# A 64-expert layer in 26 passes instead of 28: experts of different widths share a pass, and the first product moves ahead

## The reference, cut to what matters

```
scores = sigmoid(h @ w_router)                      # 64 experts
idx = top_k(scores + b_router, 8)                   # 8 experts for each token
gate[t, e] = 2.5 * scores / sum over the 8, else 0
hid = silu(h @ w_exp_gate[e]) * (h @ w_exp_up[e])   # 1024 -> 256
routed = sum_e (hid * gate[:, e]) @ w_exp_down[e]   # 256 -> 1024
ffn = routed + (silu(h @ w_sh_gate) * (h @ w_sh_up)) @ w_sh_down
```

## Time and profile before

| what | value |
|---|---|
| median of three runs | 949.46 us |
| the profiled execution's own time | 951.25 us |
| its span in the profile | 949.1 us |
| mean granted TensorE clock | 0.947 |
| TensorE busy (matmul) | 819.6 us |
| bytes moved by DMA | 279.98 MB |

### The profile page before, as it was taken

The page is one execution under the profiler, slowest core; times in us unless marked ns, Lnnn a source line. Parts: engine busy times, 40 slices in busy tenths (PEclk is TensorE's granted clock), DMA queues, the critical chain, the costliest instruction groups (busy, mean ns, idle before and its releaser), DMA issues.

```text
span 949.1 us, 10498 instructions
## 1 busy us (share of the span) xinstructions
PE 819.6 (86%) x3946; PEld 447.9 (47%) x3946; DVE 317.5 (33%) x656; ACT 154.8 (16%) x269; POOL 69.8 (7%) x64
## 2 busy tenths in 40 slices
PE   1699969988899999799999899899799897939882
PEld 0388448544455444675535445453454352505340
DVE  2120586666654427622222212212121121202116
ACT  1212342111112311211111101111111010101111
POOL 0000123344320000300000000000000000000000
PEclk9889979999999999899999989999899898969997
DMA  8962422556565277668699999999999999899901
GB/s 289 385 211 98 168 89 89 189 189 233 189 242 204 87 264 287 245 238 352 240 423 422 420 422 420 421 422 420 421 422 421 421 421 417 365 421 422 366 1 44
DMA packets 68001, 279.98 MB, mean 295 GB/s; under 512 B 8912, under 2 KB 10960, under 8 KB 43120
## 3 DMA queue, kind: packets, MB, share of 16 engines
q1 hardware_dynamic: 63888, 270.56, 71.6%
q0 software_dynamic: 2144, 5.84, 1.8%
q10 hardware_dynamic: 1920, 2.92, 0.9%
HBM read 277.69 MB, written 1.61 MB: 294 GB/s over the span
## 4 chain that ended last, share of the span: by engine, by line
PE 69%; DMA 13%; DVE 8%; issue 3%; ACT 2%; SPq 2%; POOL 2%; PEldq 0%; DVEq 0%; PEld 0%; ACTq 0%
PE bank L1694 23%; DMA up_homes<-in_w_exp_up 9%; PE bank L1720 9%; PE bank L1450 7%; PE bank L1678 5%; PE bank L1731 5%; PE bank L1457 4%; PE bank L1592 3%; PE bank L1576 3%; DMA up_homes<-in_w_ada 2%; DVE lev_e L1079 2%; PE bank L1430 2%; PE bank L1473 2%; PE bank L1602 1%; POOL lev_k L682 1%
## 5 line engine op out<-in xcount | busy, mean ns | idle before, releaser
L1694 PE MATMUL bank<-up_homes,x_g 128*64 128x512 f32 (+2 forms) x1024 | 217.5, 647 | 41.3 <-DMA up_homes<-in_w_exp_up 40.1
L1694 PEld LDWEIGHTS bank<-up_homes,x_g 128*64 128x64 f32 (+2 forms) x1024 | 72.1, 140 | 166.1 <-issue 164.4
L1457 PE MATMUL bank<-up_homes,down_homes 128*128 128x512 f32 x256 | 112.9, 594 | 2.0 <-issue 2.0
L1720 PE MATMUL bank<-down_homes,hid_t 128*32 128x512 f32 (+2 forms) x424 | 95.6, 599 | 0.7 <-ACT hid_t L912 0.7
L1324 DVE SCALAR_TENSOR_TENSOR hid<-silu_g,slot_gate,bank 128x256 f32<-128x256 f32 x29 | 13.9, 480 | 206.8 <-ACT silu_g L902 206.8
L1334 DVE TENSOR_TENSOR y_lo<-bank,y_hi 128x512 fp32r<-128x512 f32 x58 | 37.6, 687 | 119.7 <-ACT y_hi L897 119.7
L1457 PEld LDWEIGHTS bank<-up_homes,down_homes 128*128 128x128 f32 x256 | 47.4, 190 | 61.7 <-issue 61.7
L1450 PE MATMUL bank<-down_homes,up_homes 128*128 128x256 f32 x288 | 65.9, 390 | 2.3 <-DVE down_homes L1010 1.8
L1450 PEld LDWEIGHTS bank<-down_homes,up_homes 128*128 128x128 f32 x288 | 56.0, 196 | 11.3 <-issue 3.4
L682 POOL TENSOR_TENSOR lev_k<-up_homes,lev_e 128x512 f32<-128x512 f32 x28 | 47.6, 1700 | 179.7 <-ACT lev_e L828 175.7
L1678 PE MATMUL bank<-pick,h_hi 128*128 128x256 f32 x240 | 51.7, 297 | 0.0
(11 more groups left out here) (241 smaller groups left out, 793.6 us busy)
## 6 DMA issues: line engine op xcount, KB each, us to landing
up_homes<-in_w_exp_gate SPq DMA_DIRECT2D x64, 1024.0 KB, 15.0
up_homes<-in_w_exp_up SPq DMA_DIRECT2D x64, 1024.0 KB, 17.2
down_homes<-in_w_exp_down SPq DMA_DIRECT2D x53, 1024.0 KB, 17.3
up_homes<-in_w_in SPq DMA_DIRECT2D x13, 2048.0 KB, 9.1
up_homes<-in_w_ada SPq DMA_DIRECT2D x12, 2048.0 KB, 9.4
down_extra<-in_w_exp_down SPq DMA_DIRECT2D x11, 1024.0 KB, 16.4
up_homes<-in_w_out SPq DMA_DIRECT2D x2, 2048.0 KB, 10.9
up_homes<-mod_dram POOLq DMA_DIRECT2D x4, 512.0 KB, 7.1
```

The source lines that it names most:

```text
L1457: ins = mm(out[:, :], h_t[:, k, tok(h)], w[:, k, :], start=k == 0, stop=k == KD - 1)
L1694: ins = mm(gu_bank[i * m:(i + 1) * m, :].rearrange("p (b n) -> p b n", b=2), x_g[:, k, st * QUAD + i * m:st * QUAD + (i + 1) * m], w[i][:, k],
L1720: ins = mm(y_bank[h][i * m:(i + 1) * m, :], hid_t[:, f, i * m:(i + 1) * m], w[i][:, f * D + h * BANK:f * D + (h + 1) * BANK], start=f == 0 ...
```

## The change

The passes become 26. The first holds both fixed experts with 64 slots each. Of the other 25, three hold one expert (128 slots), five hold two of 64, four hold one of 96 and one of 32, and thirteen hold one of 64 and two of 32. An expert of 96 slots is computed as a tile of 64 and one of 32. So 17 passes put tiles of 64 and of 32 columns side by side. The number of loads stays 62, now with at most three in a pass. The homes are dealt in another order; the shared down weights leave the ring and go to down home 0, which pushes no up home any more; `up(0)` moves ahead of the late lists and the shared down product; VectorE makes the late lists after the first slots. The diff, cut to its core:

```diff
-SET_LOADS = [1] * FIXED + [2, 2, 4, 1] * 5 + [2, 4, 2, 4, 1, 2]
+SET_GROUPS = [[2] * FIXED] + [[2, 1, 1], [2, 2], [2, 1, 1], [3, 1], [2, 1, 1], [2, 1, 1], [4], [2, 1, 1], [2, 2],
...
+SET_LOADS = [len(groups) for groups in SET_GROUPS]
...
-    return (3, 1, 4, 2, 0)[load % UP_HOMES]
+    return (3, 0, 1, 4, 2)[load % UP_HOMES]
...
-    return load % DOWN_HOMES
+    return (load + 1) % DOWN_HOMES
...
-          + [("shared_up", 0), ("shared_down", 0)])
+          + [("shared_up", 0)])
...
+                    at = down_home(load)
                     if load >= DOWN_HOMES:
                         sp.wait_ge(y_done, 2 * (set_of(load - DOWN_HOMES) + 1))
-                    elif load == DOWN_HOMES - 1:
+                    elif at == 0:
+                        sp.wait_ge(shared_down_used, 1)
+                    elif at == DOWN_HOMES - 1:
                         sp.wait_ge(split_free, 1)
-                    elif load >= FIXED:
+                    elif at >= 2:
                         sp.wait_ge(h_lo_ready, G)
                     load_down(load, expert_of(load))
-            for s in range(FIXED):
-                ups(s)
-            sp.wait_ge(mixer_done, 4)
-            for s in range(FIXED - 1):
-                downs(s)
-            sp.wait_ge(table_ready, 1)
-            for s in range(FIXED, N_SETS):
-                ups(s)
-                downs(s - 1)
+            ups(0)
+            sp.wait_ge(mixer_done, 4)
+            sp.dma_start(shared_down, tiles(w_sh_down[0])).then_inc(shared_down_in, 16)
+            downs(0)
+            sp.wait_ge(table_ready, 1)
+            for s in range(1, N_SETS):
+                ups(s)
+                if s > 1:
+                    downs(s - 1)
...
+            def pieces(groups):
+                at = 0
+                for i, n in enumerate(groups):
+                    for m in ((2, 1) if n == 3 else (n,)):
+                        where = {} if m == JOBS else {"tile_position": (0, at * SLOTS)}
+                        yield i, slice(at * SLOTS, (at + m) * SLOTS), where
+                        at += m
...
                 for k in range(KD):
-                    for i in range(len(loads)):
-                        where = {} if m == QUAD else {"tile_position": (0, i * m)}
-                        ins = mm(gu_bank[i * m:(i + 1) * m, :].rearrange("p (b n) -> p b n", b=2),
-                                 x_g[:, k, st * QUAD + i * m:st * QUAD + (i + 1) * m], w[i][:, k],
+                    for i, slots, where in pieces(groups):
+                        ins = mm(gu_bank[slots, :].rearrange("p (b n) -> p b n", b=2),
+                                 x_g[:, k, st * QUAD + slots.start:st * QUAD + slots.stop], w[i][:, k],
                                  start=k == 0, stop=k == KD - 1, **where)
...
+            for f in range(2):
+                pe.wait_ge(*evacuated(("shared", f)))
+            up(0, 0, *loads_of(0), 1)
             pe.wait_ge(late_listed, 1)
             out = scratch_for(("late_items",))
...
-            nc.tensor.drain().then_inc(chunk_used, 1)
-            pe.wait_ge(*read_out(("late_items",)))
-            up(0, 0, *loads_of(0), 1)
+            nc.tensor.drain().then_inc(shared_down_used, 1)
             turn_hidden(0, 1)
```

More of the change, by code:

```diff
@@ L64 @@
 FIXED = 2
-SET_LOADS = [1] * FIXED + [2, 2, 4, 1] * 5 + [2, 4, 2, 4, 1, 2]
+SET_GROUPS = [[2] * FIXED] + [[2, 1, 1], [2, 2], [2, 1, 1], [3, 1], [2, 1, 1], [2, 1, 1], [4], [2, 1, 1], [2, 2],
+              [2, 1, 1], [3, 1], [2, 1, 1], [2, 1, 1], [4], [2, 1, 1], [2, 2], [2, 1, 1], [3, 1], [2, 1, 1], [2, 2],
+              [2, 1, 1], [3, 1], [2, 1, 1], [2, 2], [4]]
+SET_LOADS = [len(groups) for groups in SET_GROUPS]
 N_SETS = len(SET_LOADS)
@@ L69, with ranked @@
 FIRST_LOAD = [sum(SET_LOADS[:s]) for s in range(N_SETS + 1)]
+def ranked(at_least, at_most=JOBS):
+    return sum(at_least <= n <= at_most for groups in SET_GROUPS[1:] for n in groups)
 def set_ranks():
[L74 to L78, removed]
+    ranks = [[N_EXP - 1 - e for e in range(FIXED)]]
+    at = {n: ranked(n + 1) for n in range(1, JOBS + 1)}
+    for groups in SET_GROUPS[1:]:
+        ranks.append([])
+        for n in groups:
+            ranks[-1].append(at[n])
+            at[n] += 1
     return ranks
 SET_RANKS = set_ranks()
-JOB_RANKS = [ranks[i * len(ranks) // JOBS] for ranks in SET_RANKS for i in range(JOBS)]
-JOB_ATS = [i % (JOBS // len(ranks)) * SLOTS for ranks in SET_RANKS for i in range(JOBS)]
+JOB_RANKS = [rank for ranks, groups in zip(SET_RANKS, SET_GROUPS) for rank, n in zip(ranks, groups) for i in range(n)]
+JOB_ATS = [i * SLOTS for groups in SET_GROUPS for n in groups for i in range(n)]
 N_JOBS = len(JOB_RANKS)
-ROOM_STEPS = [(sum(n for n in SET_LOADS[FIXED:] if n == 1), 64), (sum(n for n in SET_LOADS[FIXED:] if n <= 2), 32),
-              (N_LOADS - FIXED, 32), (N_EXP - FIXED, -QUAD)]
+ROOM_STEPS = [(ranked(n + 1), SLOTS) for n in range(JOBS - 1, 0, -1)] + [(ranked(1), SLOTS), (N_EXP - FIXED, -2 * SLOTS)]
 HALF = 2 * SLOTS
@@ L136, in shape_constants @@
     put("job_at", np.array(JOB_ATS)[None].repeat(P, 0))
-    put("tie", -(np.arange(N_EXP) / N_EXP + 2.0 * TOK * (np.arange(N_EXP) < FIXED))[None].repeat(P, 0))
-    put("own_tie", -(i / N_EXP + 2.0 * TOK * (i < FIXED))[:, None])
+    fixed_last = 2.0 * TOK * np.maximum(FIXED - i, 0)
+    put("tie", -(i / N_EXP + fixed_last)[None, :N_EXP].repeat(P, 0))
+    put("own_tie", -(i / N_EXP + fixed_last)[:, None])
     put("part_no", i[:, None])
@@ L184 @@
           + [("proj_hgrn", 0), ("proj_fc", 0), ("out", 0), ("out", 1)] + [("ada", c) for c in ADA_LAST]
-          + [("shared_up", 0), ("shared_down", 0)])
+          + [("shared_up", 0)])
 CHUNK_NO = {c: n for n, c in enumerate(CHUNKS)}
-CHUNK_DMAS = {"ada": 1, "in": 1, "proj_hgrn": 1, "proj_fc": 2, "out": 1, "shared_up": 2, "shared_down": 1}
+CHUNK_DMAS = {"ada": 1, "in": 1, "proj_hgrn": 1, "proj_fc": 2, "out": 1, "shared_up": 2}
 def chunk_arrived(chunk):
@@ L401, in hybrid_layer @@
         silu_sh = moe("silu_sh", [P, TOK])
+        shared_down = down_homes[:, 0, :].rearrange("p (k n) -> p k n", k=2)
         down_home_at = [down_homes[:, 0, :], down_extra[:, :]] + [down_homes[:, n, :] for n in range(1, 5)]
@@ L474, in hybrid_layer @@
         silu_sh_ready = sem("silu_sh_ready")
+        shared_down_in, shared_down_used = sem("shared_down_in"), sem("shared_down_used")
         dve_step, act_step = sem("dve_step"), sem("act_step")
@@ L494, in scratch @@
             if use[0].startswith("late"):
-                return gu_bank
+                return o_bank[1]
             return scratch_bank[SCRATCH_NO[use] % 2]
@@ L558, in weights @@
                     sp.dma_start(by_k, tiles(w_out[0])[:, :, cols]).then_inc(s, 16)
-                elif kind == "shared_up":
+                else:
                     half = slot.rearrange("p (b k n) -> p b k n", b=2, k=KD)
@@ L562, in weights @@
                     sp.dma_start(half[:, 1], rows8(w_sh_up[0])).then_inc(s, 16)
-                else:
-                    sp.dma_start(slot[:, 0:2 * D].rearrange("p (k n) -> p k n", k=2), tiles(w_sh_down[0])).then_inc(s, 16)
             sp.dma_start(cond_t[:, 0, :], c_ctx.rearrange("(p k) -> p k", k=KD)).then_inc(cond_in, 16)
@@ L1337, in _ @@
             picks(0)
+            for f in range(2):
+                hidden_shared(f)
+            gather_out(0)
+            dve.wait_ge(split_free, 1)
+            slot_out(0, 0)
             b = awaited(("late_before",))
@@ L1346, in _ @@
             nc.vector.scalar_tensor_tensor(at_late[:, :], from_late[:, :], float(QUAD), of_late[:, :], ALU.add, ALU.mult).then_inc(late_listed, 1)
[L1347 to L1351, removed]
+            hidden(0, 0)
+            places(0, 0, 0)
             b = awaited(("late_items",))
@@ L1657, in _ @@
             pe.wait_ge(late_counted, 1)
+            for g in range(G):
+                pe.wait_ge(a_ready, g + 1)
             out = scratch_for(("late_before",))
@@ L1680, in gather, with up @@
                     ins.then_inc(gathered, 1)
-            def up(s, st, loads, times, gathered_turns):
-                m = QUAD // len(loads)
+            def pieces(groups):
[5 more added lines that the diff above has]
+                        at += m
+            def up(s, st, groups, loads, times, gathered_turns):
                 need(hid_ready, s)
@@ L1706, in turn_hidden, with down @@
                 ins.then_inc(turned, 1)
-            def down(s, loads, times, free):
-                m = QUAD // len(loads)
+            def down(s, groups, loads, times, free):
                 pe.wait_ge(hid_t_ready, val(s + 1))
@@ L1717, in down @@
                     for f in range(2):
-                        for i in range(len(loads)):
-                            where = {} if m == QUAD else {"tile_position": (0, i * m)}
-                            ins = mm(y_bank[h][i * m:(i + 1) * m, :], hid_t[:, f, i * m:(i + 1) * m],
+                        for i, slots, where in pieces(groups):
```

(15 more changed lines are left out.)

2 lines of the change are left out of this document (removed).

## The result

The changed kernel takes 1095.61 us (median of four, 1094.70 to 1096.85) against 949.42 before (four runs, 948.23 to 949.88): 1.154 times as long, interval 1.152 to 1.156. The forecast was 928.5 us in a range of 917 to 958. It is wrong; what came is the first rival, priced at 1081 us.

A forecast was written before the change was run, and what follows sets the result against it. Weights streamed by DMA bound the kernel: 17.5 (early gaps) + 2.5 (moved down load) + 3.5 (three loads a pass) − 2.5 (the end) = 21.0 us won, mixed tiles free, giving 928.5 us, range 917 to 958.

The forecast's parts named there:

- the first rival: Passes with tiles of 64 and 32: unequal tiles run one after the other, TensorE becomes the bound, 1081 us; chance 0.20.
- mixed tiles: Passes with a 64-column tile beside two of 32: low end, taken, no cost over equal tiles; high end 12.6 us more.
- the high end: Passes of unequal tiles: products cannot overlap and width changes stop the array, up 15.3 us, down 7.9, together 12.6 more.
- The second rival: Early gap closes and opens elsewhere: five up homes, six needed, SP waits in order; 938 us, chance 0.05.
- What bounds the kernel: Expert stage: the stream of weights by DMA at 421 GB/s is the bound, and TensorE fits in between.
- two passes fewer: Expert stage: 28 passes become 26, taking 30.6 us from TensorE but nothing from the time by themselves.
- The early gaps: Loads after the table, 400 to 480 us: DMA idle time falls from 26.0 to 8.5 us, so 17.5 us won.
- The part with the first up: Within the early gaps: first up starts near 416.4 and ends near 423.4, leaving one gap of 4.5 us.
- The second fixed down load: SP's queue: 1 MiB moved ahead of the table into idle time, 2.5 us won, nobody held up.
- At most three loads in a pass: Two up homes always free to fill, so the dry queue from 800 to 820 us goes: 3.5 us won.
- The clock behind the last wait: Up at the last weight wait took 10.03 us, not 7.00: up to 3.0 could come back, nothing taken.
- The late pass: Expert 1's tokens beyond its 64 slots: one late pass before and after, nothing won or lost.

The follow-up runs named there:

- e3: Changed kernel with the up's products ordered by width, all 64-column tiles and then all 32-column tiles, one change of width inside an up: 1061.43 us.
- e1: Changed kernel with every pass of unequal groups computed in tiles of 32 columns only; plan, loads and order stay: 933.74 us, 0.981 of before.
- e7: Order of e1 with another plan of 26 passes, each of one width, including eight passes of four experts: 951.23 us, 1.000 of before.
- e5: Kernel of e1 with the second fixed expert's down load behind the table instead of ahead of it: 929.82 us, 0.979 of before.
- e4: Kernel of e1 with the first up put back behind the late lists and the shared down product, VectorE's lists meant to come earlier: 946.85 us, 0.996 of before.
- e6: Kernel of e1 with SP waiting for the last bias row before it asks for the second fixed down load, still ahead of the table: 929.79 us, 0.977 of before.
- e1_again: The kernel of e1 unchanged, run again as the base for the second group of runs: 933.34 us.

## Why the prediction was wrong

**The step that failed** is "I take the low end" under mixed tiles: that a pass with a tile of 64 beside two of 32 costs what a pass of equal tiles costs. It costs 13.2 us more; the high end of the same paragraph was 12.6. I had read every change of width in the trace as a conflict over columns, because all of them landed on columns in use, and took the neighbours of the earlier trace rows as the nearest rows. They were nearest in place, not in width, and width decides. With 17 passes the term was worth 225 us against a gain of 21, so the nearest row was too thin a ground for a chance of 0.70 against 0.20. The rule of the Trainium skill, TensorEngine Tiling (Array Packing), section Tiling Modes, that a change of tiling mode and not only of tile drains TensorE, agrees with the after trace (0.81 us in which the load for other columns is held) and with the 0.13 us that e3 gives a change. What costs most, that tiles of 64 and 32 overlap in none of these passes, is what that rule leads to.

**The first rival** was right in mechanism, price and point: TensorE becomes the bound at 4.7 us a mixed pass, and at 13.2 it is. Its sum of 1081 lacks 0.6 us for each of 17 passes, 10 us, and some 2 us by which the second up came later (434.65 against 432.8); that leaves 2 to 3. The sum of the second rival is a us short (928.5 + 3.5 + 7 is 939, not 938); nothing hangs on it.

**What bounds the kernel** was right, and e1 shows it: with the widths out of the way weights are the bound at 421 GB/s. That two passes fewer are worth nothing by themselves has no run of its own; e7, with 26 passes too, is no faster than before. The forecast's 928.5 us is meant for the kernel of e1, and there the sum can be redone by its own working. From 400 to 480 us 351 GB/s leave 13.3 us lost, not 8.5, so 12.7 are won, not 17.5; the 3.5 at 800 us are won (419 GB/s), and 2.5 goes in and out. That is 16.2 us, and the spans of before and e1 differ by 16.2 (949.1 − 932.9). On that kernel, then, the sum misses by the size of one term. That e5 lands at 929.8, and its last wait at 826.94 beside the 827.7 put down, is in part luck: it lacks the load ahead of the table, and part of its gain is not explained.

**The early gaps** were thus sized 4.8 us too large, of which the bias row is 2.7. The part with the first up accounts for some 8.5 of the 13.1 us that e4 gave back, as large as put down (13 instead of 4.5), and the loads after the table went out in the order worked out.

**The second fixed down load** was wrong in sign: "nobody is held up" held for SP and missed POOL's queue. The 1 MiB made the bias row 2.4 to 2.7 us later and with it the routing and every load, as much as the 2.5 us it was to win; without the collision e5 and e6 were 3.5 us faster, more than the row alone explains (2.2 us of it in e6; in e5 2.7, less 2.5 of stream).

**At most three loads in a pass** was too small for its place. The 3.5 us were what 28 passes lost that way; with 26 passes of one width e7 loses 17.9 us against e1_again. Rival 2 names this mechanism; it struck the plan that I had not priced.

**The clock behind the last wait** I took at nothing, with 3.0 as bound: behind the shorter wait the up still took 8.58 us in e1, at a granted clock of 0.82, 9.45 and 0.74 in e1_again, 9.54 and 0.74 in e5; before it was 10.03 and 0.70. Between 0.5 and 1.5 of the 3.0 came back.

**The late pass** stayed one, as counted.

## What to carry to other kernels

In these traces column tiles ran beside tiles of their own width only, shown for 64 and 32 in fp32: where experts of different widths share a pass, cut all of them to the narrowest width and let a wide expert's weights stream through two tiles; four narrow tiles cost no more (7.00 us an up against 7.02). When a term rests on a case the trace does not show and its two ends differ by ten times the gain, the sum is a bet on that case; measure it by itself first. And a transfer put into an idle stretch is only free if no small transfer on the path, on any queue, shares that stretch.

## What the runs showed of the hardware

Tiles of 64 and 32 columns on disjoint columns do not run together: the load for the second width is held for 0.81 us, about the length of the first tile's product in a step (0.86). A change of width costs 0.13 us beyond that. Four tiles of 32, two of them with the same weights, take 7.00 us like one product of 128 columns (6.87). A row of 4 KB on POOL's queue takes 4.46 to 4.74 us instead of 1.97 to 2.09 when SP's queue asks for 1 MiB in the same moment. An up of four tiles takes 7.00 us at a granted clock of 1.00 (2.4 GHz); behind a wait for weights it took 10.03 at a mean of 0.70 and 8.58 at 0.82, in proportion.
